# Sums of the down product's weight blocks moved from accumulating DMAs to GpSimd in SBUF

## The reference, cut to what matters

```
h2 = rms_norm(x, norm_mlp)
x = x + jnp.square(jax.nn.relu(h2 @ w_ff1)) @ w_ff2     # (512,1024)@(1024,4096), (512,4096)@(4096,1024)
return rms_norm(x, norm_final)
```

## Time and profile before

| | |
|---|---|
| device time, median of three | 1694.51 us (1692.86 to 1695.10) |
| the profiled execution | 1691.07 us, its span 1689.3 us |
| TensorE busy | 1665.4 us, 99% of the span |
| VectorE busy | 960.4 us, 57% |
| ScalarE busy | 678.5 us, 40% |
| GpSimd busy | 112.0 us, 7% |
| granted TensorE clock, mean | 0.998 of full speed |
| accumulating queue (q0, software_dynamic) | 26.23 MB, 8.0% of 16 engines |
| plain queue (q1, hardware_dynamic) | 325.95 MB, 50.0% |

### The profile page before, as it was taken

How to read it: one execution, slowest core, us unless ns; L and a number is a source line. 1 busy time by engine, 2 the same in 40 slices (tenths; PEclk the granted TensorE clock), 3 DMA queues, 4 the chain that set the end, 5 groups by cost and what they waited for, 6 DMA issues and landing times.

```text
span 1689.3 us, 24245 instructions
## 1 busy us (share of the span) xinstructions
PE 1665.4 (99%) x9882; PEld 1232.6 (73%) x9882; DVE 960.4 (57%) x1280; ACT 678.5 (40%) x847; POOL 112.0 (7%) x168
## 2 busy tenths in 40 slices
PE   9999999999999999999999999999999999899998
PEld 7888888865444535453588877778888889779986
DVE  6424438452343334324568755567675578778887
ACT  6334433321111101111366633344642367756775
POOL 4000000000000000000011012210000001100100
PEclk9999999999999999999999999999999999999999
DMA  7332223948999999999541332124352339767864
GB/s 272 102 98 76 75 75 100 353 190 344 428 428 429 428 428 428 428 428 428 198 151 54 100 100 73 54 76 130 109 188 100 104 130 242 161 184 210 206 132 130
DMA packets 90712, 353.43 MB, mean 209 GB/s; under 512 B 7856, under 2 KB 7872, under 8 KB 78208
## 3 DMA queue, kind: packets, MB, share of 16 engines
q1 hardware_dynamic: 78288, 325.95, 50.0%
q0 software_dynamic: 12336, 26.23, 8.0%
HBM read 345.87 MB, written 6.29 MB: 208 GB/s over the span
## 4 chain that ended last, share of the span: by engine, by line
PE 92%; DMA 3%; DVE 2%; ACT 2%; issue 1%; POOL 0%; DVEq 0%; ACTq 0%; POOLq 0%
PE bank L3097 41%; PE bank L3450 12%; PE bank L3874 8%; PE bank L3463 7%; PE bank L3899 6%; PE bank L3358 4%; PE bank L3398 3%; PE bank L3630 2%; PE bank L3122 2%; PE bank L3143 1%; DMA ring<-in_w 1%; DMA b_one<-in_w_ff 1%; DMA w_stage<-in_w_ff 1%; PE bank L3660 1%; PE bank L3683 1%; DVE down L2020 1%
## 5 line engine op out<-in xcount | busy, mean ns | idle before, releaser
L3097 PE MATMUL bank<-act_hi,w_hi 128*128 128x512 f32 x768 | 302.8, 394 | 0.0
L3097 PE MATMUL bank<-act_hi,w_lo 128*128 128x512 f32 x768 | 299.2, 390 | 0.0
L3097 PE MATMUL bank<-act_lo,w_hi 128*128 128x512 f32 x768 | 299.0, 389 | 0.0
L2005 DVE TENSOR_TENSOR w_lo<-w_stage,w_hi 128x2048 fp32r<-128x2048 f32 x65 | 148.9, 2290 | 152.1 <-ACT w_hi L1187 152.1
L3450 PE MATMUL bank<-ring,xgT 128*64 128x512 f32 x992 | 216.1, 592 | 1.4 <-ACT xgT L1409 1.4
L1187 ACT ACTIVATE w_hi<-w_stage 128x2048 fp32r<-128x2048 f32 x65 | 124.7, 1918 | 198.6 <-PE bank L3097 187.6
L3450 PEld LDWEIGHTS bank<-ring,xgT 128*64 128x64 f32 x992 | 71.0, 137 | 142.6 <-issue 139.6
L3097 PEld LDWEIGHTS bank<-act_hi,w_hi 128*128 128x128 f32 x768 | 144.2, 188 | 32.2 <-issue 2.9
L3097 PEld LDWEIGHTS bank<-act_hi,w_lo 128*128 128x128 f32 x768 | 144.1, 188 | 30.4
L3097 PEld LDWEIGHTS bank<-act_lo,w_hi 128*128 128x128 f32 x768 | 144.3, 188 | 29.0
L3899 PE MATMUL bank<-down,part_hi 128*128 128x512 f32 x448 | 138.6, 391 | 5.6 <-DVE down L2020 4.4
(11 more groups left out here) (539 smaller groups left out, 3033.9 us busy)
## 6 DMA issues: line engine op xcount, KB each, us to landing
ring<-in_w SPq DMA_DIRECT2D x94, 2048.0 KB, 16.4
w_stage<-in_w_in SPq DMA_DIRECT2D x42, 1024.0 KB, 5.1
w_stage<-in_w_ff SPq DMA_DIRECT2D x19, 1024.0 KB, 6.6
b_sum<-in_w_ff POOLq DMA_DIRECT2D x12, 1024.0 KB, 9.5
w_stage<-in_w_out SPq DMA_DIRECT2D x8, 1024.0 KB, 5.0
b_one<-in_w_ff SPq DMA_DIRECT2D x6, 1024.0 KB, 8.2
stage<-in_w_ff SPq DMA_DIRECT2D x5, 1024.0 KB, 6.5
branch_gates<-gate_out POOLq DMA_DIRECT2D x16, 256.0 KB, 2.6
```

What stands on the lines that cost most here:

```text
L2005: dve.tensor_tensor(w_lo[s][:, 0:ktiles, :], w_stage[s][:, 0:ktiles, :], w_hi[s][:, 0:ktiles, :].bitcast(F32), ALU.subtract).then_inc(w_lo ...
L3097: ins = pe.matmul(banks[j][:, :], left, right, start=(kc == 0 and k == 0 and n_pass == 0), stop=(kc == g.chunks - 1 and k == g.ktiles - 1 ...
```

## The change

Three of the four weight sums are now additions and subtractions on GpSimd, SBUF to SBUF (`pool.tensor_tensor`, 128x2048), from blocks that SyncE loads plainly. b_one[1] and b_far are loaded with B22 instead of B12, and GpSimd subtracts b_sum (B12) from them. b_sum is loaded anew with B11 (`load_firsts`), and GpSimd adds b_one[1] or b_far. w_stage is loaded with B22 (`load_lasts`), and GpSimd subtracts b_sum. That is six operations a half, counted by `sum_made`. Only the fourth sum keeps its negation and its accumulating DMA. `b_negated` counts 2 a half instead of 8, `b_added` 1 a buffer instead of 5.

Four orders change with it: `load_ones` moves ahead by one block load, the loads of blocks (4, 0) and (5, 0) move behind the second b_one load, `mlp_squares` runs before the first splits and not among them (with the first squares of unit 0 spread around the third product's split), and in the last unit of a half ADD_22 stands ahead of `part_split_lo(h, 0)`. The relu of unit 0 uses blk_fifth and blk_last instead of blk_first and blk_both.

```diff
-        SUM_LOADS, STAGE_LOADS, ONE_LOADS, ADDS, NEGATED = 1, 2, 2, 5, 8
+        SUM_LOADS, ONE_LOADS, ADDS, NEGATED = 2, 2, 1, 2
...
-        relu_t = (blk_first, blk_both)
+        relu_t = (blk_fifth, blk_last)
...
+        def made(h, n, kc):
+            return 2 + 6 * h + n + kc + 1
...
-                sp.dma_start(b_one[1][:, :, :], weight_block(h, 0, 1, 0)).then_inc(b_one_in[1], 16)
-                sp.dma_start(b_far[:, :, :], weight_block(h, 0, 1, 1)).then_inc(b_one_in[0], 16)
+                sp.dma_start(b_one[1][:, :, :], weight_block(h, 1, 1, 0)).then_inc(b_one_in[1], 16)
+                sp.dma_start(b_far[:, :, :], weight_block(h, 1, 1, 1)).then_inc(b_one_in[0], 16)
+
+            def load_firsts(h):
+                for kc in range(2):
+                    sp.wait_ge(sum_made, made(h, THIRD_MADE, kc))
+                    sp.dma_start(b_sum[kc][:, :, :], weight_block(h, 0, 0, kc)).then_inc(b_sum_in[kc], 16)
+
+            def load_lasts(h):
+                for kc in range(2):
+                    sp.wait_ge(w_lo_done, step(h, 2 + kc))
+                    sp.dma_start(w_stage[kc][:, :, :], weight_block(h, 1, 1, kc)).then_inc(w_loaded[kc], 16)
...
             load_blocks(2, 1)
+            load_ones(0)
             unit_split(1)
             load_blocks(3, 0)
-            load_ones(0)
             third_made(2)
             load_blocks(3, 1)
+            load_firsts(0)
             unit_split(2)
...
                 load_step(0, 2 + kc)
+            load_lasts(0)
...
-            sp.wait_ge(w_lo_done, step(0, 7))
-            load_blocks(4, 0)
-            load_blocks(5, 0)
             sp.wait_ge(w_lo_done, step(0, 8))
             sp.dma_start(b_one[1][:, :, :], weight_block(0, 1, 1, 1)).then_inc(b_one_in[1], 16)
+            load_blocks(4, 0)
             sp.wait_ge(pe_tiles, 4 * (g_down[0].chunk0 + 12))
             load_blocks(4, 1)
+            load_blocks(5, 0)
...
-                    pool.wait_ge(b_negated, NEGATED * h + kc + 1)
-                    add_block(h, kc, 1, b_sum[kc], weight_block(h, 1, 1, kc))
-                    add_block(h, kc, 2, b_sum[kc], weight_block(h, 0, 0, kc))
...
+                    pool.wait_ge(b_sum_in[kc], loaded(h, "sum", 1))
+                    pool.wait_ge(b_one_in[1 - kc], loaded(h, "one", 1))
+                    pool.tensor_tensor(far_blocks[kc][:, :, :], far_blocks[kc][:, :, :], b_sum[kc][:, :, :], ALU.subtract)\
+                        .then_inc(sum_made, 1)
+                for kc in range(2):
+                    pool.wait_ge(b_sum_in[kc], loaded(h, "sum", 2))
+                    pool.wait_ge(sum_made, made(h, THIRD_MADE, kc))
+                    pool.tensor_tensor(b_sum[kc][:, :, :], b_sum[kc][:, :, :], far_blocks[kc][:, :, :], ALU.add)\
+                        .then_inc(sum_made, 1)
+                for kc in range(2):
+                    pool.wait_ge(*stage_in(f"t{kc}", h)[1:])
+                    pool.wait_ge(sum_made, made(h, SECOND_MADE, kc))
+                    pool.tensor_tensor(w_stage[kc][:, :, :], w_stage[kc][:, :, :], b_sum[kc][:, :, :], ALU.subtract)\
+                        .then_inc(sum_made, 1)
...
             split_hi(g_up.chunk0 + 1, 1)
+            for t in range(NT):
+                mlp_squares(t)
+            own.settle()
+            act.sem_inc(n_sd, NT)
             t_high(T2)
             t_high(T3)
-            for t in range(2):
-                mlp_squares(t)
...
-                    if u in (1, 2):
-                        negate_sums(u - 1)
-                    elif u in (4, 5):
-                        negate_sums(u - 4)
-                    elif u in (3, 6):
-                        for kc, block in enumerate((b_one[1], b_far)):
-                            act.wait_ge(b_one_in[1 - kc], loaded(h, "one", 1))
-                            negate(block, block)
...
                     slot_low(u, 6)
+                    blk_add(u, ADD_22, 4, CP_FIFTH, blk_fifth, first)
                     if closing:
                         part_split_lo(h, 0)
-                    blk_add(u, ADD_22, 4, CP_FIFTH, blk_fifth, first)
-                    if closing:
                         step_split_lo(h, 0)
```

More of the change, by code:

```diff
@@ L489, in two_blocks @@
         far_loaded, raw_copied = extra_in, hg_log
+        sum_made = low_pad
         hid_summed, b_negated = sem("hid_summed"), sem("b_negated")
@@ L591, in weight_block @@
             return A["w_ff2_2"][0][rows, q * 512:(q + 1) * 512].rearrange("(k p) n -> p k n", p=P)
+        THIRD_MADE, SECOND_MADE, FIRST_MADE = 0, 2, 4
+        def made(h, n, kc):
+            return 2 + 6 * h + n + kc + 1
         def early(t):
@@ L972, in _ @@
             load_blocks(5, 1)
+            load_ones(1)
             unit_split(4)
             load_blocks(6, 0)
-            load_ones(1)
             third_made(5)
             load_blocks(6, 1)
+            load_firsts(1)
             unit_split(5)
@@ L988, in _ @@
                 load_step(1, 2 + kc)
+            load_lasts(1)
             sp.wait_ge(part_low, V_PARTS + PARTS + 3)
@@ L1153, in _ @@
             pool.sem_inc(r_pool, 1)
-            def add_block(h, kc, k, dst, block):
-                pool.wait_ge(b_added[kc], loaded(h, "added", k - 1))
-                pool.dma_start(dst[:, :, :], block, accum_op=ALU.add).then_inc(b_added[kc], 16)
             for h in range(HALVES):
+                far_blocks = (b_one[1], b_far)
+                for kc in range(2):
[8 more added lines that the diff above has]
+                        .then_inc(sum_made, 1)
+                for kc in range(2):
+                    pool.wait_ge(*stage_in(f"t{kc}", h)[1:])
+                    pool.wait_ge(sum_made, made(h, SECOND_MADE, kc))
+                    pool.tensor_tensor(w_stage[kc][:, :, :], w_stage[kc][:, :, :], b_sum[kc][:, :, :], ALU.subtract)\
+                        .then_inc(sum_made, 1)
                 for kc in range(2):
                     pool.wait_ge(b_negated, NEGATED * h + kc + 1)
-                    add_block(h, kc, 1, b_sum[kc], weight_block(h, 1, 1, kc))
-                    add_block(h, kc, 2, b_sum[kc], weight_block(h, 0, 0, kc))
[L1165 to L1173, removed]
+                    pool.dma_start(b_sum[kc][:, :, :], weight_block(h, 1, 0, kc), accum_op=ALU.add)\
+                        .then_inc(b_added[kc], 16)
         @block.scalar
@@ L1852, in step_split_hi @@
                     act.wait_ge(b_one_in[v % 2], loaded(h, "one", 2))
+                elif v < 10:
+                    act.wait_ge(sum_made, made(h, {2: SECOND_MADE, 3: FIRST_MADE, 4: THIRD_MADE}[v // 2], v % 2))
                 else:
-                    act.wait_ge(b_added[v % 2], loaded(h, "added", {2: 2, 3: 4, 4: 3, 6: 5}[v // 2]))
+                    act.wait_ge(b_added[v % 2], loaded(h, "added", 1))
                 act.wait_ge(pe_tiles, (g_down[h].chunk0 + v - 1 - (v == 0)) * 4)
@@ L1862, in _, with first_squares @@
             split_hi(g_up.chunk0 + 1, 1)
+            for t in range(NT):
+                mlp_squares(t)
+            own.settle()
+            act.sem_inc(n_sd, NT)
             t_high(T2)
             t_high(T3)
-            for t in range(2):
-                mlp_squares(t)
             slot_high(1, 0)
             slot_high(1, 1)
-            for j in range(4):
+            def first_squares(j):
                 act.wait_ge(pe_tiles, (g_up.chunk0 + 1) * 4 + j + 1)
@@ L1875, in _ @@
                 act.activation(hidden[:, j, :], relu_t[j % 2][:, :], ACT.Square).then_inc(hid_sq, 1)
-                if j in (1, 2):
-                    mlp_squares(j + 1)
-            own.settle()
-            act.sem_inc(n_sd, NT)
-            def negate_sums(kc):
-                act.wait_ge(b_sum_in[kc], loaded(kc_half[kc], "sum", 1))
-                negate(b_sum[kc], b_sum[kc])
-                kc_half[kc] += 1
-            kc_half = [0, 0]
+            t_high(T1)
+            for j in range(3):
+                first_squares(j)
             def up_units(h):
@@ L1894, in up_units @@
                     slot_high(u, 2)
-                    if first:
-                        t_high(T3 if h else T1, h)
+                    if u == 1:
+                        first_squares(3)
+                    elif first:
+                        t_high(T3, h)
                     copy_first(u)
@@ L1945, in _ @@
                     part_split_hi(h, n + 2)
-                    if n == 0:
-                        act.wait_ge(w_lo_done, step(h, 2))
-                        act.wait_ge(b_added[0], loaded(h, "added", 2))
-                        negate(w_stage[0], b_sum[0])
                     step_split_hi(h, 2 * n + 4)
-                    if n == 0:
-                        act.wait_ge(w_lo_done, step(h, 3))
-                        act.wait_ge(b_added[1], loaded(h, "added", 2))
-                        negate(w_stage[1], b_sum[1])
-                    elif n in (1, 2):
+                    if n in (1, 2):
                         act.wait_ge(w_lo_done, step(h, n + 3))
```

(1 more changed line is left out.)

10 lines of the change are left out of this document (4 added, 6 removed).

## The result

The kernel after takes 1721.29 us (median of runs from 1719.85 to 1722.49), the kernel before took 1693.68 in the runs beside it: the ratio is 1.0162, with an interval of 1.0143 to 1.0181. The change makes the kernel 27.6 us slower. The profiled execution has a span of 1718.0 us, 28.7 more than before.

The account below looks back on a forecast made before the run. TensorE's own work and few idle moments were taken to bound the kernel. Loss of 26.8 us from six pairs less 9.0 gained gave +17.8 on the median 1694.5, so 1712.3 us; range 1686 to 1725.

Parts of the forecast that it names:

- The ceiling of the gain: TensorE's idle time in the last 310 us, the squared-ReLU product: at most 9.07 us to win.
- (a): ADD_22 put ahead of the activation split, into VectorE's 0.99 us gap: the idle at 1437 and 1602 returns, 2.6 us.
- (b): 12 of 16 ScalarE negations go, two before down step 1's split: the idle of 1446 to 1463 returns, 4.5 us.
- (c): First half, loads for blocks 4 and 5 moved behind the load that took 14.08 us: idle at 1507 returns, 1.0 us.
- (d): Sums of squares put in ScalarE's 4.75 us idle before 1369: the third product's split comes earlier, 0.8 us back.
- The rival in which the plain loads keep the late landings: Eight plain loads bunched with step loads; only ADD_22's 2.6 and the start's 0.8 us come: about 1692, chance 0.07.
- The length of an addition: Each of GpSimd's twelve 128x2048 additions with both operands in SBUF takes 4.0 us, with ends 2.0 and 6.1.
- The hold: GpSimd and VectorE take turns, the second waiting until the other ends; a pair of additions holds VectorE for 8.0 us.
- What TensorE can bear: Per pair, lead, VectorE idle and bank additions absorb 3.9 us up, 2.8 down; left 4.1 and 5.2, total 26.8.
- Covers: Waits on GpSimd's sums, in SyncE's load_firsts and ScalarE's step splits 4 to 9: covered except at the upper end.

## Why the prediction came out as it did

The direction and the mechanism were right; the loss was 27.6 us and not 17.8.

**The ceiling of the gain, 9.07 us.** Right as idle time: 8.9 came back, and all the stretches of the earlier trace rows are closed. In device time the same edits gave 13.5, of which 1.7 is the overlap that a stop takes away, 2 lie before the product, and the rest is no more than the executions differ by.

**Its parts.** (a) 2.6 us for ADD_22: right about the stops, wrong as a gain of its own; alone it gave 1.0 us, which its interval doesn't tell from nothing, as the 1.2 at 1437 moved to the next wait and the clock took back the 1.4 at 1602. (b) 4.5 us: right that two negations stood in front of down step 1, and moving them (with ADD_22's order) brought it. (c) and (d) are tested only together with these: the run with these orders left 1.1 us of idle. The squares do fit ScalarE's gap: they start at 1364.5 in the kernel after and t_hi at 1369.37, as against 1369.16. The rival in which the plain loads keep the late landings is out: with the sums cut to four columns the same loads left 0.2 us of idle.

**The length of an addition, 4.0 us.** Too short. The first takes 4.90 us, of which some 0.4 is its wait for the VectorE instruction before it (1393.73 + 1.22 against 1394.54), so about 4.5 by itself. The error came from doubling the select's slope exactly; the real ratio of two operands to one is 4.5 to 2.04. "GPSIMD Engine Reference" of the Trainium skill (Performance versus the Vector engine) has 4497 ns for it, and the trace agrees.

**The hold.** Right in kind: VectorE waits for GpSimd's instruction to end, and GpSimd for VectorE's, whole instructions in turn. VectorE's busy time rose by 42.0 us, 3.5 per addition, since an addition that starts first holds a VectorE instruction only for what is left of it when that one comes. The Trainium skill ("SBUF — State Buffer", Who interferes with whom) says that such a VectorE instruction and a GpSimd one that reads SBUF exclude one another, and leaves those that only write out of it; the write-only run (no hold) and the one-operand run (a hold of 1.7 and 1.1 us in the rows shown) agree with both halves. My reading that bank additions run on was right too (0.69 us at 1395.52). The row at 37.66, where VectorE made eight subtractions without giving GpSimd a turn, stands against strict turns; no run here explains it.

**What TensorE can bear.** Forecast up 4.1 us and down 5.2 of idle per pair; measured on average (5.66 + 5.67 + 5.66 + 2.56) / 4 = 4.9 and (3.52 + 3.72) / 2 = 3.6. The sum, 26.8, is the forecast's 26.8, but that is luck: the errors cancel. Up, I counted VectorE's mean idle (1.9 us) and the bank addition (0.7) as absorbing. In three of the four pairs they don't: the hold falls wholly between the pair's start and the third product's split, and what that split has is its lead. "Delay less lead" gives 5.8 where TensorE stood 5.66, and 1.38 in the run with one sum of each pair where it stood 1.26. The fourth pair starts one split earlier in its unit, and its hold falls on the splits of the first two products of the next unit. VectorE's timeline there:

```profile
1579.81 4.39 DVE L2025 TENSOR_TENSOR slot_lo<-stage,slot_hi 128x1024 fp32r<-128x1024 f32 x1 [0.40 <-ACT slot_hi L1812]
...
1584.73 5.00 DVE L2025 TENSOR_TENSOR slot_lo<-w_stage,slot_hi 128x1024 fp32r<-128x1024 f32 x1
```

The two are held for 6.9 us together, of which some 1.1 goes into idle time that VectorE has around a bank addition between them; and in the kernel with no sums the second of them has a lead of 3.2 us (it ends at 1573.23, its product starts at 1576.47). 5.8 less 3.2 is 2.6, and TensorE stood 2.39. So the rule holds there too, but where in the unit a pair falls decides whose lead counts, and with it half of the idle time. Down, the same rule would give more than was measured. VectorE's timeline there, after:

```profile
1472.07 5.39 DVE L2025 TENSOR_TENSOR down<-b_sum,down 128x2048 fp32r<-128x2048 f32 x1 [0.57 <-ACT down L1878]
...
1478.05 5.99 DVE L2963 TENSOR_TENSOR hidden<-s_two,hidden 128x2048 f32<-128x2048 f32 x1
```

The first delay, 3.1 us, falls on the split that TensorE needs next and costs 2.11 us (3.1 less a lead of 0.94); the second, 3.7 us, falls on `hidden`, and the split that stands behind it comes 1.41 us too late.

**The missing term: the clock.** I had the granted clock at 1.00 in all stretches and no step for what stops do to it. TensorE's stretches behind the stops, after:

```profile
1409.80:1414.10 4.30, 4.30 (x25) 0.66 0.17 18
1414.10:1430.00 15.90, 15.90 (x134) 1.00 0.71 261
1437.20:1441.40 4.20, 4.20 (x24) 0.66 0.08 4
1477.60:1481.00 3.40, 3.40 (x8) 0.50 0.02 5
1567.10:1572.00 4.90, 4.84 (x22) 0.50 0.15 36
1590.50:1594.00 3.50, 3.50 (x19) 0.55 0.00 0
1654.50:1658.00 3.50, 3.50 (x11) 0.59 0.02 5
...
1663.00:1667.00 4.00, 4.00 (x19) 1.00 0.00 0
```

The second row is the measure for up: 134 matmuls in 15.90 us are 0.119 each at 2.4 GHz, so the 25 of the row before it should take 2.97 and took 4.30: 1.3 us lost. In the down product 19 in 4.00 (the last row) make 1.7 for the eight at 1477.60, which took 3.40 at 1.2 GHz: 1.7 us lost. There are six such places in the product, one behind each pair's first stop; read in stretches of 1 us, the granted clock is at 1.2 GHz for some 3.4 us in five of them and for 6.8 in the one at 1567. Half of 5 x 3.4 + 6.8 is 11.9 us, of which 0.9 falls into the stops themselves, where it costs nothing: 11.0. Busy time rose by 10.8 against the kernel before, whose own stops cost overlap too, and by 12.4 against the kernel with no sums, of which 1.4 would be lost overlap. The trace of the kernel before has no such place in the product, though TensorE stands for up to 3.0 us at a time. So what the prediction's sum lacked is a term for the clock: stops of 26.8 us carried some 11 us of it with them. With that term it is 17.8 + 10.8 = 28.6 us, by which the product did grow. (The medians are 27.6 apart, the two profiled executions' spans 28.7.)

The kernel before isn't free of this in every execution. Its trace has a mean granted clock of 0.998; of 23 others, the three at 0.999 took 1689.97 to 1690.67 us and the five at 0.996 took 1694.61 to 1696.24. No trace of these was kept, so where their clock fell isn't shown.

**Covers.** SyncE's load_firsts waiting on GpSimd's sums cost nothing: TensorE's waits over the product, after, name no transfer. The profile puts one wait of a ScalarE split down to a sum, 3.5 us at 1651; the same split of the first half waits as long for TensorE, so the sum isn't what held it.

```profile
PE bank L3878 <- DVE slot_lo L2025: 19.5, 5, 5.7
PE bank L3903 <- issue: 4.4, 2, 2.3
PE bank L3903 <- DVE down L2025: 2.8, 2, 1.4
```

(What is waited for: us in total, times, longest.) The two put down to "issue" are the first stops of the down pairs. The trace names no releaser for them; that they belong to the held splits rests on the timeline above and on their absence without the sums.

## What to carry to other kernels

Before work is moved to GpSimd, look at what VectorE does beside it: an SBUF-to-SBUF addition there holds VectorE for nearly its whole length (3.5 us of 4.5 on average), in turns of whole instructions, and if VectorE's splits feed TensorE, the price is that delay less the lead of the next split that it falls on, plus what the clock loses behind the stop. Price an idle moment of the bounding engine by what it waits for last: the 9 us here were to be had by changes of order, with no arithmetic moved, and one of them alone gave 1.0 us, which its interval doesn't tell from nothing. When a change has a part that reorders and a part that moves work, run them apart.

## What the runs showed of the chip that I had not expected

- Stops of TensorE of 2.1 to 5.7 us cost more than themselves: six stretches at 1.2 GHz behind them, 1.3 and 1.7 us lost in the two worked out above, some 11 us in all. The length of the stop alone doesn't decide it. With the first sum of each pair alone the four up stops of 1.26 to 1.68 us left the clock at 1.00, and the two down stops of 2.2 and 2.3 us were followed by 0.50. With ADD_22's order alone the clock fell at the stop at 1460 (5.00 us at 0.50 behind it), while the trace of the kernel before, which stood for 3.0 us there, kept 1.00; and cutting the sums in four shortened the up stops and left the clock's loss as it was. What decides it stays open.
- GpSimd and VectorE alternate instruction by instruction even when one is half as long as the other (1.1 us beside 2.28): 2.96 us per quarter on GpSimd, 3.38 us per subtraction on VectorE. So cutting GpSimd's work up saved 6.5 us of idle and 6.0 of the product's length, no more.
- On GpSimd, 128x2048 elements of float32 take 1.82 us to write (memset), some 2.0 to read and write (select), and about 4.5 with a second operand (addition). Of these the memset didn't hold VectorE, and the other two did.
